# The second block's projections, branch gates and output projection as three passes of high and low parts

## The chip, the cores and the metric

The program runs on one core of a Trainium2 chip. The metric is the device time of one execution, in microseconds. The engines are TensorE (PE; its weight loads are PEld), VectorE (DVE), ScalarE (ACT), GpSimd (POOL) and SyncE (SP, which here only starts transfers).

## What is computed

Two blocks follow one another on x, 512 tokens by 1024 columns, all in float32. The first block has two layers of attention (three kinds of heads) and a gated feed-forward network (FFN). The change is in the second block, cut here to what matters:

```python
u   = modulate(rms_norm(x, norm1_g), sh1, sc1)            # 512 tokens
u_c = modulate(rms_norm(ctx, norm1_g), sh1c, sc1c)        # 256 tokens of context
p, pc = split_cols(u @ w_in), split_cols(u_c @ w_in)
# p[0:4] GLA q, k, v, gate; p[4] 32 columns of decay ranks; p[5:9] mLSTM q, k, v, gate;
# p[9] 16 columns of gates; p[10] 2 x 1024 branch gates
o = bidirectional(gla_scan, ...)                          # 4 heads, dk 128, dv 256, chunks of 64
h = bidirectional(mlstm_scan, ... to_colmajor(p[j]) ...)  # 4 heads, tokens in column order
y_gla = head_rms_norm(o) * silu(p[3])
y_m   = from_colmajor(head_rms_norm(h)) * sigmoid(p[8])
gate_gla, gate_m = split(sigmoid(p[10]))
y = gate_gla * (y_gla @ w_br_gla) + gate_m * (y_m @ w_br_mlstm)
x = x + g1 * (y @ w_out)
x = x + g2 * swiglu(modulate(rms_norm(x, norm2_g), sh2, sc2), w_ffn_in, w_ffn_out)
return rms_norm(x, final_g)
```

Each of the two directions of a scan runs over the context first and then over the 512 tokens. The largest matrix products have a contraction of 1024, that is eight k tiles of 128.

## The kernel before

Every engine has its own instruction list, written out in order by one Python function per engine; semaphores order the engines among each other. There is no planner.

In the first block, and in the FFN of both blocks, a float32 product is three matmuls on numbers in the type fp32r: an operand a is split into a high part (a rounded to fp32r) and a low part (a minus its high part, rounded to fp32r), and high x high + high x low + low x high are added up in PSUM. In the second block, from its projections to its output projection, the products are plain fp32 matmuls on x and weights as they come. `mm` (L754) issues every matmul.

The weights of the second block come over the SyncE queue (`load`, L1405, which walks through `second_pieces`, L473) into three slots of `ring`, each of 4096 columns; a piece holds q, k and v of a head, or its gate, or the four 128-column parts of one branch step, or half of the output weights. TensorE goes in this order:

- It transposes ctx, sums the squares of ctx (`norm_sums`), spreads the inverse roots, computes the 32 decay-rank columns for x and for ctx, then the eleven projections of GLA head 0 (`PROJECTIONS`, L497: q; k of the context, ("k", 0); k of x, ("k", 1); six 128-token tiles of v, two of the context and four of x; two gate tiles of 128 columns).
- In each of the four GLA heads it does the decay inputs of this head and, put between them and the two scans (`gla_scan`, L1217), the projections of the next head: q behind the first decay inputs, both k and v 0 and 1 behind the second, v 2 behind the first scan's key transposes, v 3 between the state updates, v 4 behind them, v 5 and a gate in the second scan, the other gate ahead of `head_outputs`. A generator per unit (`steps` in `projections`, L1161) lets single k tiles be placed between other matmuls.
- In GLA head 3 these are the projections of mLSTM head 0, on x in column order. GpSimd permutes four of the eight k tiles of the normed x and VectorE the other four (`permute`, L562).
- Then the 16 gate columns, the gate rows (running sums and maxima on four partitions, on VectorE), q and k of mLSTM head 1, and the four mLSTM heads (`mlstm_scan`, L1306), again with the next head's projections between. Head 3 has no next head.
- The branch stage: for each of eight column tiles a gate (`branch_gates`, L1347), the product of the GLA output with its branch weights, a second gate, the product of the mLSTM output. Then eight jobs of the output projection, and the FFN.

ScalarE moves the results out of PSUM in the same order (`evacuate`, L1747), between the decay exponentials (`decay_exponents`, L1772: a chain of activations that waits for VectorE's running sums) and the head's norm. In it q of the next head is evacuated inside the first direction's chain, ("k", 0) inside the second's, and ("k", 1) and v behind it. VectorE norms x and ctx (`norm_apply`), makes the decays, the states, the state updates out of PSUM, and the products with the gates. GpSimd has little to do in the second block: it starts the transfer of ctx, permutes, and subtracts for the first FFN piece (`first_low`, L666).

Of the kernel before, what the change touches and what calls it, by code (L numbers as in the profile page):

```python
# [81 lines left out]
def build(nc, A, out):  # L82
    ctx = ExitStack()
    with ctx:
# [8 lines left out]
        spare = sb("spare", [P, 2, KT * P])  # L93
# [49 lines left out]
        with ExitStack() as mixing:  # L143
            U = mixing.enter_context(nc.sbuf_tensor("U", [P, KT, 768], F32))
            R = mixing.enter_context(nc.sbuf_tensor("R", [P, 26624], F32))
            ring = mixing.enter_context(nc.sbuf_tensor("ring", [P, NSLOT, SLOT], F32))

        with ExitStack() as parts:
# [3 lines left out]
            ring_parts = parts.enter_context(nc.sbuf_tensor("ring_parts", [P, NSLOT, SLOT], mybir.dt.float32r))  # L152
        with ExitStack() as stacked:
            stacked.enter_context(nc.sbuf_tensor("U_under", [P, KT, 768], F32))
            stacked.enter_context(nc.sbuf_tensor("R_under", [P, QK_AT], F32))
            QKP = stacked.enter_context(nc.sbuf_tensor("QK_parts", [P, 20, S], mybir.dt.float32r))
        xn = U[:, :, 256:768]
# [12 lines left out]
        wL = sb("wL", [P, 2, FP], FR)  # L170

# [142 lines left out]
        ctxin = R[:, 14208:16256].rearrange("p (t c) -> p t c", t=CT)  # L314
        ctxT = R[:, 16256:18304].rearrange("p (k c) -> p k c", k=KT)
        U0 = U[:, :, 0:256]
# [32 lines left out]
        setup = sem("setup")  # L349
        sq_ready, folded = sem("sq_ready"), sem("folded")  # L350
# [122 lines left out]
        def second_pieces():  # L473
            w = A["w_in_2"][0]
            yield lambda i: [(slot(i, KT, 32), cols(w, O_LR, O_LR + 32))]
            for o in (O_GLA, O_ML):
                for h in range(NH2):
                    if o is O_ML and h == 1:
                        yield lambda i: [(slot(i, KT, 16), cols(w, O_GATES, O_GATES + 16))]
                    gate = lambda i, h=h, o=o: [(slot(i, KT, DV), cols(w, o[3] + h * DV, o[3] + (h + 1) * DV))]  # L480
                    if o is O_ML and h == 0:
                        yield gate
                    yield lambda i, h=h, o=o: [
                        (slot(i, KT, DK, 0), cols(w, o[0] + h * DK, o[0] + (h + 1) * DK)),
                        (slot(i, KT, DK, KT * DK), cols(w, o[1] + h * DK, o[1] + (h + 1) * DK)),
                        (slot(i, KT, DV, 2 * KT * DK), cols(w, o[2] + h * DV, o[2] + (h + 1) * DV))]
                    if o is O_GLA or h > 0:
                        yield gate
            for m in range(KT):
                yield lambda i, m=m: [  # L490
                    (slot(i, KT, P, n * KT * P), cols(src, a + m * P, a + (m + 1) * P))
                    for n, (src, a) in enumerate(((w, O_BR), (A["w_br_gla_2"][0], 0), (w, O_BR + D), (A["w_br_mlstm_2"][0], 0)))]
            for j in range(2):
                yield lambda i, j=j: [(slot(i, KT, 512), cols(A["w_out_2"][0], j * 512, (j + 1) * 512))]


        PROJECTIONS = [("q", 0), ("k", 0), ("k", 1)] + [("v", t) for t in range(6)] + [("gate", 0), ("gate", 1)]  # L497
# [59 lines left out]
        vtmp2 = R[:, 12288:12800].rearrange("p (a c) -> p a c", a=1)  # L557
        BR = R[:, 8192:8192 + 4096].rearrange("p (k c) -> p k c", k=KT)
# [3 lines left out]
        def permute(pg, e, k, scratch):  # L562

            pg.do(e.tensor_copy(scratch.rearrange("p (c r) -> p c r", r=8), xn[:, k, :].rearrange("p (r c) -> p c r", c=64)))
            pg.do(e.tensor_copy(xn[:, k, :], scratch))
# [13 lines left out]
        def _(pool):  # L579
# [143 lines left out]
            pg.more(x_ready, KT)  # L723
            pool.dma_start(ctxin, A["ctx_2"][0].rearrange("(t p) c -> p t c", p=P)).then_inc(ctx_in, 16)
# [6 lines left out]
            pg.seen[sq_ready] = (2 * L + 1) * KT  # L731
# [7 lines left out]
        def _(pe):  # L739
# [38 lines left out]

            def norm_sums(src, nt, ks, bank=None):

                if bank is None:
                    bank = ab.fill(pe)
                for k in ks:
                    pp.more(sq_ready)
                    for t in range(nt):

                        ins = nc.tensor.matmul(bank[:, t:t + 1], src(k)[:, t * P:(t + 1) * P], ones[:, 0:1],
                                               start=k == 0 and t == 0, stop=k == KT - 1, skip_group_check=True)
                    if k == KT - 1:
                        ins.then_inc(a_full, 1)  # L790
                return bank
# [343 lines left out]
            Xc = lambda k: U0[:, k, :]  # L1135

# [3 lines left out]

            spread_roots(S)
            pe.wait_ge(ctx_in, 16)
# [7 lines left out]
            norm_sums(Xc, CT, range(KT))  # L1150
            spread_roots(256)
            pp.more(xn_ready, KT)
            i = weights()
# [1292 lines left out]
```

## Time and profile before

| | us |
|---|---|
| median of 3 runs | 3038.78 |
| lowest and highest of them | 3037.37, 3041.61 |
| the profiled execution | 3035.83 |
| its span (first to last instruction) | 3034.0 |
| TensorE busy in the span | 2849.8 (94%) |
| second block, ahead of its FFN | 1579 to 2627 |

The profile is of one execution, and all positions below are microseconds from the start of its span. A record of the timeline joins instructions that follow one another: it shows the start, the time to the end of the last, the engine, line and operation, output and inputs by name with their sizes, the count, and in brackets the idle time before it with what ended it. "PE L754 ... x32" is 32 matmuls. An fp32 matmul leaves two records, one in fp32r leaves one. PEclk is the granted TensorE clock as a share of full speed.

### The profile page before, as it was taken

The numbers are of one execution on the slowest core, as the hardware profiler recorded it, in microseconds if no ns is written. First come the engines' busy times: TensorE is split into PE (matmuls) and PEld (weight loads), VectorE is DVE, ScalarE is ACT, GpSimd is POOL, SyncE is SP. The second block draws the span as 40 slices with busy tenths as digits, with TensorE's granted clock in tenths as the row PEclk, the third lists the DMA queues.
The fourth block names the chain that finished last, engine by engine and source line by source line (L and its number), as shares of the span: only waits on it lengthen the run. The fifth ranks groups of instructions, "written<-read, shape, count | busy, mean of one in ns | idle before, by whom it ended". The sixth has DMA issues, their size and how long they took to land.

```text
span 3034.0 us, 33407 instructions
## 1 busy us (share of the span) xinstructions
PE 2849.8 (94%) x13064; PEld 2038.8 (67%) x13064; DVE 1240.7 (41%) x1736; ACT 972.5 (32%) x1634; POOL 753.7 (25%) x600
## 2 busy tenths in 40 slices
PE   7988999999999899999989999798998999899997
PEld 6866668887896675888765555446665444488886
DVE  2758445443263853554231333425333100333322
ACT  5468422222344861222221334332222000122221
POOL 5565403346544650234650000100000000100000
PEclk9999999999999999999999999899998999899999
DMA  5230024545422002455551110111112231133331
GB/s 126 91 64 1 19 82 123 138 131 142 122 86 85 5 18 56 111 138 135 142 154 49 42 39 18 29 31 53 35 35 56 56 83 56 42 97 98 90 95 66
DMA packets 383948, 230.26 MB, mean 76 GB/s; under 512 B 9292, under 2 KB 378060, under 8 KB 383792
## 3 DMA queue, kind: packets, MB, share of 16 engines
q1 hardware_dynamic: 381040, 223.04, 26.5%
q0 software_dynamic: 2224, 2.99, 0.9%
q8 instruction: 104, 1.70, 0.2%
q10 hardware_dynamic: 528, 2.10, 0.2%
q14 instruction: 52, 0.43, 0.0%
HBM read 226.01 MB, written 2.10 MB: 75 GB/s over the span
## 4 chain that ended last, share of the span: by engine, by line
PE 76%; ACT 8%; DVE 7%; DMA 6%; issue 2%; POOL 0%; SPq 0%; ACTq 0%; DVEq 0%; POOLq 0%
PE ps L754 65%; PE scores L754 8%; DMA raws<-in_w_down 5%; PE ps L910 1%; ACT wH L1685 1%; DVE R L1957 1%; DVE spare L1967 0%; ACT spare L1547 0%; ACT U L1524 0%; DMA ring<-in_w_in 0%; ACT R L1552 0%; DVE QK_parts L1947 0%; ACT R L1520 0%; PE ps L858 0%; ACT U_parts L1476 0%
## 5 line engine op out<-in xcount | busy, mean ns | idle before, releaser
L754 PE MATMUL ps<-xH,wH 128*128 128x512 f32 x992 | 391.5, 395 | 0.0
L754 PE MATMUL ps<-xH,wL 128*128 128x512 f32 x992 | 386.5, 390 | 0.0
L754 PE MATMUL ps<-xL,wH 128*128 128x512 f32 x992 | 386.1, 389 | 0.0
L1685 ACT ACTIVATE wH<-raws 128x2048 fp32r<-128x2048 f32 (+1 forms) x114 | 192.9, 1692 | 504.3 <-PE ps L754 312.1
L2154 DVE TENSOR_TENSOR wL<-raws,wH 128x2048 fp32r<-128x2048 f32 (+1 forms) x113 | 233.0, 2062 | 280.5 <-ACT wH L1685 280.4
L754 PE MATMUL ps<-R 128*64 128x128 f32 (+6 forms) x1768 | 272.6, 342 | 30.3 <-issue 4.5
L754 PE MATMUL ps<-U,ring 128*128 128x512 f32 (+4 forms) x640 | 269.3, 573 | 8.2 <-ACT R L1767 8.2
L754 PE MATMUL ps<-R,ring 128*128 128x512 f32 x624 | 271.3, 593 | 2.9 <-DVE R L2378 1.6
L663 POOL TENSOR_TENSOR U<-U 128x512 f32<-128x512 f32 x12 | 19.5, 1627 | 1023.4 <-ACT U L1480 1023.4
L754 PEld LDWEIGHTS ps<-R 128*64 128x64 f32 (+2 forms) x1768 | 171.1, 165 | 147.3 <-issue 86.9
L680 POOL TENSOR_TENSOR spare<-spare,cvec 128x1024 f32<-128x1024 f32 x64 | 125.3, 1958 | 560.5 <-DMA spare<-in_w_ada 560.5
L754 PE MATMUL ps<-ring_parts,U_parts 128*128 128x256 f32 (+1 forms) x1440 | 208.1, 284 | 12.9 <-DVE ring_parts L2009 6.7
L754 PEld LDWEIGHTS ps<-R,ring 128*128 128x128 f32 x624 | 118.2, 190 | 151.6 <-issue 147.7
L754 PEld LDWEIGHTS ps<-xH,wL 128*128 128x128 f32 x992 | 186.3, 188 | 39.7
L754 PEld LDWEIGHTS ps<-U,ring 128*128 128x128 f32 (+2 forms) x640 | 118.2, 188 | 140.8 <-issue 125.1
L754 PEld LDWEIGHTS ps<-xL,wH 128*128 128x128 f32 x992 | 186.5, 188 | 38.9 <-issue 1.0
L754 PEld LDWEIGHTS ps<-xH,wH 128*128 128x128 f32 x992 | 186.5, 188 | 38.3 <-issue 1.0
L754 PE MATMUL ps<-hH,wH 128*128 128x512 f32 x528 | 209.9, 398 | 1.5 <-DVE wL L2154 1.5
L754 PE MATMUL ps<-hH,wL 128*128 128x512 f32 x528 | 207.0, 392 | 0.0
L754 PE MATMUL ps<-hL,wH 128*128 128x512 f32 x528 | 206.8, 392 | 0.0
L754 PEld LDWEIGHTS ps<-ring_parts,U_parts 128*128 128x128 f32 x1440 | 193.9, 194 | 14.1 <-issue 11.8
L682 POOL TENSOR_TENSOR spare<-spare 128x512 f32<-128x512 f32 (+2 forms) x192 | 198.3, 1033 | 15.0
(367 smaller groups left out, 4159.2 us busy)
## 6 DMA issues: line engine op xcount, KB each, us to landing
raws<-in_w_gate_up SPq DMA_DIRECT2D x88, 512.0 KB, 5.5
ring<-in_w_in SPq DMA_DIRECT2D x34, 1024.0 KB, 6.3
spare<-in_w_ada SPq DMA_DIRECT2D x64, 512.0 KB, 4.1
raws<-in_w_down SPq DMA_DIRECT2D x32, 704.0 KB, 6.1
raws<-in_w_ffn_in SPq DMA_DIRECT2D x44, 512.0 KB, 5.1
ring<-in_w_in SPq DMA_DIRECT2D x32, 512.0 KB, 6.2
raws<-in_w_ffn_out SPq DMA_DIRECT2D x16, 704.0 KB, 4.6
ring<-in_w_o SPq DMA_DIRECT2D x6, 896.0 KB, 5.6
```

What stands on the lines that cost most here:

```text
L663: pg.do(nc.gpsimd.tensor_tensor(xn[:, 0, :], xn[:, 0, :], xn[:, k, :], ALU.add), folded)
L680: pg.do(nc.gpsimd.tensor_tensor(w_, w_, bc(cvec[:, :, ADA[a][1]], P, 2), ALU.mult))
L682: pg.do(nc.gpsimd.tensor_tensor(w[:, 0:n_ * P], w[:, 0:n_ * P], w[:, n_ * P:2 * n_ * P], ALU.add), ada_summed if n_ == 1 else None)
L754: return nc.tensor.matmul(o, a, b, start=first, stop=last)
L910: ins = nc.tensor.transpose(bank[:, s_ * P:(s_ + 1) * P], PX[a % 4][:, c, s_ * P:(s_ + 1) * P], ident[:, :])
L1685: ap.do(f(wH[:, g % 2, 0:n], raws[:, g % 2, 0:n], ACT.Copy), wh_ready)
L1957: vp.do(v.tensor_reduce(nmax[:, n:n + 2], SP[a % 2][:, :, :], AX.X, ALU.max, negate=True), s_max)
L2154: vp.do(v.tensor_tensor(wL[:, g % 2, 0:n], raws[:, g % 2, 0:n], wH[:, g % 2, 0:n].bitcast(F32), ALU.subtract), wl_ready)
```

## The change

The second block's projections, narrow jobs, branch gates and output projection become three passes of high and low parts. The two products of the branch stage with w_br_gla and w_br_mlstm stay plain fp32.

- The weights come in 36 pieces of 128 x 2048 (256 columns for each of eight k tiles): q and k of a head, v, gate, in this order by head (v and gate of mLSTM head 0 ahead of its q and k), then eight pairs of branch gates and four quarters of the output weights. A piece goes to place 0 or 1 in turn (`PLACE`), and from the branch stage on to places 0, 2, 3, of which 2 and 3 lie in `R`. A place holds the raw piece, and its high and low parts in `ring_parts` or `R_parts`.
- ScalarE rounds piece j + 1 (`second_part`) behind an evacuation of piece j: behind the second unit of a q/k or v piece, behind the first of a gate piece; in the branch stage behind every second gate. GpSimd makes all low parts (`split_piece`), and both parts of the 32 and 16 narrow columns (`split_small`).
- x is normed into a high part (`x_high`, ScalarE) and a low part (`u_low`, VectorE). ctx is normed ahead of its transposes, by ScalarE (squares with a sum, root, scaled copy), and ScalarE writes it twice out of PSUM; VectorE subtracts.
- `permute` copies both parts of each k tile. `PROJECTIONS` goes q, ("k", 1), ("k", 0). In the entry the rank columns of the context come behind q and k of x.
- The branch sums are split into `BR_HIGH` and `BR_LOW`. The first FFN piece of the second block waits for the last piece in place 0 (the second output quarter) instead of the last output weights.

The diff, cut to its core:

```diff
+        SECOND = ([(name, h) for h in range(NH2) for name in ("qk", "v", "gate")]
+                  + [("v", NH2), ("gate", NH2), ("qk", NH2)]
+                  + [(name, h) for h in range(NH2 + 1, 2 * NH2) for name in ("qk", "v", "gate")])
+        N_PROJ = len(SECOND)
+        SECOND += [("branch", m) for m in range(KT)] + [("out", j) for j in range(4)]
+        PLACE = [j % 2 for j in range(N_PROJ)] + [(0, 2, 3)[j % 3] for j in range(KT + 4)]
-        PROJECTIONS = [("q", 0), ("k", 0), ("k", 1)] + ...
+        PROJECTIONS = [("q", 0), ("k", 1), ("k", 0)] + ...
@@ permute (GpSimd and VectorE)
-            pg.do(e.tensor_copy(scratch.rearrange(...), xn[:, k, :].rearrange(...)))
-            pg.do(e.tensor_copy(xn[:, k, :], scratch))
+            for part in (x_high(k), u_low(k)):
+                pg.do(e.tensor_copy(scratch.rearrange(...), part.bitcast(F32).rearrange(...)))
+                pg.do(e.tensor_copy(part, scratch))
@@ GpSimd
+            def split_piece(j):
+                raw_, high, low = place_parts(PLACE[j])
+                if j == 0:
+                    pool.wait_ge(piece_in[0], 16 * len(second_dmas(0)))
+                    pg.do(nc.gpsimd.tensor_copy(high, raw_))
+                else:
+                    pool.wait_ge(second_high, j)
+                pg.do(nc.gpsimd.tensor_tensor(low, raw_, high.bitcast(F32), ALU.subtract), piece_split)
+            for j in range(4, SECOND.index(("gate", NH2))):
+                split_piece(j)
             pool.wait_ge(head_in, NH2)
             for k in range(POOL_TILES):
                 permute(pg, nc.gpsimd, k, ptile)
             pg.also(u_permuted)
+            for j in range(SECOND.index(("gate", NH2)), len(SECOND)):
+                split_piece(j)
@@ TensorE
+            def parts_steps(o, a, b, on_tile=None):
+                for k in range(KT):
+                    if on_tile:
+                        on_tile()
+                    (ah, al), (bh, bl) = a(k), b(k)
+                    mm(o, ah, bh, k == 0, False)
+                    mm(o, ah, bl, False, False)
+                    yield mm(o, al, bh, False, k == KT - 1)
@@ projections, steps
-                    i = at_slot[part]
+                    j = SECOND.index(("qk" if name in "qk" else name, h))
+                    pe.wait_ge(piece_split, j + 1)
                     bank = ab.fill(pe)
...
+                    for ins in parts_steps(o, a, b):
+                        done = ins
                         yield
+                    done.then_inc(a_full, 1)
+                    read_second[j] = (a_full, ab.n)
@@ branch gates and output
+                j = N_PROJ + m
+                pe.wait_ge(piece_split, j + 1)
+                parts_job(ab, lambda b: b[:, :], piece_columns(j, n * P, P), XP)
...
+                parts_job(db, lambda b: b[:, :], piece_columns(j, m % 2 * P, P), lambda k: (BR_HIGH[:, k, :], BR_LOW[:, k, :]))
@@ SyncE
+            def load_second(j):
+                i = PLACE[j]
+                if last[i] is not None:
+                    sp.wait_ge(*read_second[last[i]])
...
+                for dst, src in second_dmas(j):
+                    sp.dma_start(dst, src).then_inc(piece_in[i], 16)
@@ ScalarE
+            def second_part(j):
+                i = PLACE[j]
+                landed[i] += 16 * len(second_dmas(j))
+                act.wait_ge(piece_in[i], landed[i])
+                raw_, high, _ = place_parts(i)
+                ap.do(f(high, raw_, ACT.Copy), second_high)
             def evacuate(h, *jobs):
...
+                    evacuate_one(h, name, m)
+                    j = SECOND.index(("qk" if name in "qk" else name, h))
+                    units[j] += 1
+                    if units[j] == (1 if name == "gate" else 2):
+                        second_part(j + 1)
@@ ScalarE, branch gates
                 ap.also(gate_ready)
+                if n % 2 or n == 2 * KT - 2:
+                    second_part(N_PROJ + (n + 1) // 2 + (n >= 2 * KT - 2))
@@ VectorE
-            norm_apply(lambda k: gm[:, 0, k:k + 1], lambda k: mod[:, sh1 + k, 0:1])
-            vp.more(ctx_ready)
-            norm_apply(lambda k: gm[:, 1, k:k + 1], lambda k: mod[:, sh1 + k, 1:2], U0, ctxT, CT)
+            norm_into_parts(lambda k: gm[:, 0, k:k + 1], lambda k: mod[:, sh1 + k, 0:1], u_low, x_high, context_root)
+            for k in range(0, KT, 2):
+                two = slice(k, k + 2)
+                vp.do(v.tensor_tensor(spare_parts[:, two, :], ctxT[:, two, :], UP[:, two, 0:256].bitcast(F32), ALU.subtract), xn_ready)
...
-                vp.do(v.tensor_tensor(BR[:, m, :], BR[:, m, :], vtmp2[:, 0, :], ALU.add), br_ready)
+                vp.do(v.tensor_tensor(PTb[:, 0, :], PTb[:, 0, :], PTb[:, 1, :], ALU.add))
+                split(BR_HIGH[:, m, :], BR_LOW[:, m, :], PTb[:, 0, :], br_ready)
```

## Rows read from the trace of the kernel before

**Rows 1.** the page's busy time by engine: us, share of the span, instructions

```profile
PE 2849.8 (94%) x13064; PEld 2038.8 (67%) x13064; DVE 1240.7 (41%) x1736; ACT 972.5 (32%) x1634; POOL 753.7 (25%) x600
```

**Rows 2.** windows view: stretch, us, busy us (xcount) of PE, PEld, DVE, ACT, POOL, PEclk, DMA, GB/s

```profile
1603.00:1668.10 65.10, 64.35 (x210) 37.12 (x209) 8.34 (x19) 7.33 (x14) 0.00 (x0) 0.97 0.18 49
1842.00:1928.50 86.50, 80.41 (x313) 46.82 (x312) 32.36 (x54) 31.87 (x51) 0.00 (x0) 0.98 0.13 37
1928.50:2010.60 82.10, 62.96 (x266) 37.70 (x266) 37.31 (x62) 30.34 (x48) 7.64 (x8) 0.88 0.01 1
...
2137.30:2218.80 81.50, 78.95 (x307) 51.33 (x306) 28.19 (x71) 19.15 (x35) 0.00 (x0) 1.00 0.14 39
2363.00:2570.00 207.00, 205.39 (x479) 90.63 (x477) 15.98 (x24) 10.46 (x17) 0.00 (x0) 1.00 0.26 71
```

**Rows 3.** timeline, matmuls: start us, us, engine line operation, xcount [idle before <-releaser]

```profile
2570.01 55.20 PE L754 MATMUL ps<-R,ring 128*128 128x512 f32 x128 [1.62 <-DVE R L2378]
...
1643.08 7.07 PE L754 MATMUL ps<-ring,U 128*128 128x256 f32 x32
...
2700.11 0.39 PE L754 MATMUL ps<-xH,wH 128*128 128x512 f32 x1
...
2702.83 0.39 PE L754 MATMUL ps<-xH,wH 128*128 128x512 f32 x1
...
60.48 1.84 PE L754 MATMUL ps<-ring_parts,U_parts 128*128 128x256 f32 x14
62.16 0.28 PE L754 MATMUL ps<-ring_parts,xL 128*128 128x256 f32 x1
```

**Rows 4.** groups by line and form, the splitting of weights: xcount, busy us, mean ns

```profile
L1472 ACT ACTIVATE ring_parts<-ring 128x2048 fp32r<-128x2048 f32 x18 | 34.5, 1917 | 6.3 <-DMA ring<-in_w_in 5.4 <-DVE wL L2154 0.3
...
L643 POOL TENSOR_TENSOR ring_parts<-ring,ring_parts 128x2048 fp32r<-128x2048 f32 x17 | 79.1, 4653 | 85.4 <-ACT ring_parts L1472 85.1
```

**Rows 5.** timeline of the head at 1842 us

```profile
1842.02 0.69 PE L754 MATMUL ps<-R,C 32*128 32x256 f32 x2
...
1856.32 12.21 PE L754 MATMUL ps<-U,ring 128*128 128x256 f32 x32 [4.19 <-ACT R L1767]
...
1869.29 0.39 ACT L1524 ACTIVATE R<-ps 128x256 f32<-128x256 f32 x1
...
1875.27 1.05 PE L754 MATMUL ps<-R 128*128 128x128 f32 x8
...
1902.79 0.70 PE L754 MATMUL ps<-R 64*128 64x256 f32 x4
...
1915.76 4.89 PE L754 MATMUL ps<-R 128*128 128x256 f32 x24 [0.75 <-DVEq L56]
...
1920.58 7.13 PE L754 MATMUL ps<-U,ring 128*128 128x512 f32 x16
...
1925.33 1.52 DVE L2250 TENSOR_SCALAR R<-R,rsg 128x256 f32<-128x256 f32 x4
```

**Rows 6.** timeline at the start of the last feed-forward network

```profile
2631.57 1.91 ACT L1685 ACTIVATE wH<-raws 128x2048 fp32r<-128x2048 f32 x1 [3.22 <-PE ps L754]
...
2632.41 0.49 DVE L2135 TENSOR_SCALAR R<-R,mod 128x512 f32<-128x512 f32 x1
...
2633.62 4.50 POOL L670 TENSOR_TENSOR wL<-raws,wH 128x2048 fp32r<-128x2048 f32 x1 [12.30 <-ACT wH L1685]
...
2633.72 4.68 DVE L2135 TENSOR_SCALAR R<-R,mod 128x512 f32<-128x512 f32 x1
```

**Rows 7.** timeline at the permutation

```profile
1944.39 0.60 DVE L564 COPY R<-U 128x512 f32<-128x512 f32 x1
...
1948.86 8.61 PE L754 MATMUL ps<-ring,U 128*128 128x256 f32 x32 [17.25 <-DVEq L56]
```

**Rows 8.** timeline at the end of the gate rows

```profile
2069.60 1.01 PE L1303 MATMUL ps<-ident,R 4*128 4x4 f32 x8 [6.83 <-ACT R L1844]
```

**Rows 9.** timeline of the mLSTM head at 2137 us

```profile
2170.72 0.69 DVE L2352 TENSOR_TENSOR R<-R 128x512 f32<-128x512 f32 x1 [2.09 <-ACT R L1864]
```

More of the change, by code:

```diff
@@ new lines, in second_dmas @@
+        def second_dmas(j):
+            (name, h), w = SECOND[j], A["w_in_2"][0]
+            dst = place_parts(PLACE[j])[0]
+            if name == "branch":
+                return [(dst[:, :, n * P:(n + 1) * P], cols(w, O_BR + n * D + h * P, O_BR + n * D + (h + 1) * P)) for n in range(2)]
+            if name == "out":
+                return [(dst, cols(A["w_out_2"][0], h * 256, (h + 1) * 256))]
+            o, h = (O_GLA, O_ML)[h // NH2], h % NH2
+            if name == "qk":
+                return [(dst[:, :, n * DK:(n + 1) * DK], cols(w, o[n] + h * DK, o[n] + (h + 1) * DK)) for n in range(2)]
+            n = 2 if name == "v" else 3
+            return [(dst, cols(w, o[n] + h * DV, o[n] + (h + 1) * DV))]
@@ L498, in build, with branch_raw @@
+        read_second, branch_read = [None] * len(SECOND), []
+        def branch_raw(m, n):
+            return slot(1, KT, P, m % 2 * (SLOT // 2) + n * KT * P)
+        PROJECTIONS = [("q", 0), ("k", 1), ("k", 0)] + [("v", t) for t in range(6)] + [("gate", 0), ("gate", 1)]
         N_CONST = 4 + L * (6 + 1 + 4)
@@ L777, in _ @@
             pe.wait_ge(setup, 2)
[L779 to L791, printed above, removed]
             def two_sums(bank, total, last):
@@ L1254, in head_outputs @@
                     ins.then_inc(d_full, 1)
-            first = projections()
-            for name, m in PROJECTIONS:
+            first = projections(0)
+            for name, m in PROJECTIONS[:2]:
+                run(first(name, m))
+            pp.more(xn_ready, KT // 2)
+            parts_job(ab, lambda b: b[0:32, 0:256], small(LR_AT, 2 * RANK), XcP)
+            pe.wait_ge(tab_in, 80)
+            for name, m in PROJECTIONS[2:]:
                 run(first(name, m))
@@ L1278, in _ @@
                 head_outputs()
[L1281 to L1285 removed]
+            pe.wait_ge(gates_split, 1)
+            parts_job(ab, lambda b: b[0:16, 0:256], small(GATES_AT, 16), XcP)
+            parts_job(ab, lambda b: b[0:16, :], small(GATES_AT, 16), XP)
             gates_out = ab.n
@@ L1413, in load_ffn @@
                 up_down = FFN_W[l]
-                sp.wait_ge(*read_by[base + (before[l] - base - 1) // NSLOT * NSLOT])
+                if l < L:
+                    sp.wait_ge(*read_by[base + (before[l] - base - 1) // NSLOT * NSLOT])
+                else:
+                    sp.wait_ge(*read_second[max(j for j in range(len(SECOND)) if PLACE[j] == 0)])
                 for q in range(NF):
```

301 lines of the change are left out of this document (169 added, 132 removed).

## The prediction

> **What bounds the kernel now.** I read the page first: TensorE is busy for 94% of the span [rows 1]. Then I cut the second block (1579 to 2627 us) into stages with the windows view [rows 2]: in the first projections and the branch stage the matmul records fill the window (64.35 of 65.1 us, 205.39 of 207). In the scan stages they nearly do (80.41 of 86.5 us in a GLA head, 78.95 of 81.5 in an mLSTM head), and only around the permutation is there a hole (62.96 of 82.1). So a cheaper matmul shortens the first kind of stage one for one. In a scan stage one has to follow the chain: there projections fill the time in which ScalarE and VectorE work on the decays.
>
> The prices [rows 3]: an fp32 matmul is two records, one of 512 columns 55.20/128 = 0.43 us, so 0.86 per k tile; one of 256 columns 7.07/32 = 0.22, so 0.44. In fp32r, 512 columns come every 2.72/12 = 0.227 us, three passes 0.68; 256 columns every 1.68/14 = 0.12, three passes 0.36. A k tile of 512 columns gains 0.18, one of 256 gains 0.08.
>
> **The change, part by part.** Each of eight heads has 32 k tiles of 512 columns (q, k, two gates) and 56 of 256 (k of the context, six v): 5.8 + 4.5 = 10.3 us less matmul, 82 in all. Sixteen branch gates (128 k tiles) give 23, the output projection (64) 11.5, the two narrow jobs 4: 121 us of work leave TensorE. What is added per 1 MB piece of weights stands between its landing and its first matmul: ScalarE's rounding, 1.92 us, and GpSimd's subtraction, 4.65 [rows 4], for 36 pieces. Neither engine is full (ScalarE 31.9 of 86.5 us in a head [rows 2]). What counts is where in ScalarE's order the rounding stands.
>
> *Entry.* x is now normed into two parts, so VectorE's last tile comes at about 1605 to 1607 instead of 1596 (an estimate: one more 128x512 subtraction per tile, 0.69 as in [rows 9], and collisions with GpSimd, below), but TensorE no longer waits for the context's norm before x's jobs. Behind it stand q and k of x (2 x 5.4), the narrow job and k of the context (2 x 2.9), six v (17.3), two gates (10.9): 44.8, and some 4 for the first v piece (rounded only after two evacuations) and a slow clock: head 0 begins at 1656, not 1668. -12, bounds -17 (no collision) and -6.
>
> *GLA heads 0 to 2.* This is where I expect the work saved to be lost. A head begins at 1842.02 [rows 5]. Its k of the context waits 4.19 us for ScalarE's evacuation of q, which stands behind the decay chain, and k's own evacuation comes at 1869.29, 27.3 us into the head: ScalarE reaches it by its exponentials, not by TensorE's. The rounding of the next head's v piece now stands right behind that evacuation, and TensorE's v job waits for rounding and subtraction: 27.7 + 1.9 + 4.6 = 34.2 us into the head. In the kernel before both first v jobs were done at 33.25 (1875.27). TensorE now idles from about 25 to 34.2, and such an idle time brings the slow clock: after the 4.19 us wait, 32 records of 256 and 512 columns took 12.21 us for the 10.4 that [rows 3] give. So v0 and v1 (5.8, and 2 for the clock) end at 42, 8.7 later than before. Back come: v2 0.6, the scan with v3 and v4 1.7, v5 0.6, the second scan with a gate between its pairs (1902.79 to 1915.76, 13 us) 2.2. The last gate's 1.5 is mostly not regained: the head's norm chain ends at 1926.85, 6.3 after that gate starts, and the gate now takes 5.4. That is 5.7 back of 8.7: each head +3, three heads +9. Bounds: 0 (the clock stays up and the chain starts earlier, since ScalarE evacuates the last gate sooner) and +18 (6 a head).
>
> *GLA head 3.* The permutation copies both parts: GpSimd's 7.64 us [rows 2] and VectorE's 4.4 (1944.39 to 1948.8, the end of TensorE's 17.25 us wait [rows 7]) double, and VectorE starts later behind GpSimd's copies: +6. The rest of the head returns 5.5. Sum +0.5, bounds -5 and +3.
>
> *Gate rows.* The narrow jobs and q start the chain 3.7 earlier. But from about 2041 VectorE works through scans and row operations without a pause, and TensorE waits for the end of it (2069.60, 6.83 idle [rows 8]). Two subtractions (q/k and v of mLSTM head 1) fall into this stretch. That GpSimd holds VectorE up is in the trace: while GpSimd subtracted for 4.50 us, a VectorE operation that began 0.10 later took 4.68 where its like took 0.49 [rows 6]. Two such stops cost up to 9. Sum +5, bounds -4 (no stop) and +6.
>
> The Trainium skill (SBUF — State Buffer, on the port pair that VectorE and GpSimd share) says that the pair is an exclusive lock, held for the whole instruction, against VectorE operations in a two-port mode or with two SBUF inputs. By that rule the scans and additions of the gate rows are stopped as the one above was, and those that read PSUM are not; without it this stage would be -4 instead of +5 and the forecast some 15 us lower.
>
> *mLSTM heads 0 to 2.* Here q and k are evacuated without a chain before them, so v is rounded at 9 and subtracted at 15.5 us into the head; v0 starts 15.6 in, 17.2 before. The gate piece's subtraction then covers VectorE's multiplication of the scores (2170.72, 33.4 into the head [rows 9]), which without it would come 3 us earlier. I get: second direction starting 3.8 earlier, its v jobs and gate another 2.8, the last gate lost to the norm chain as above: -6.5 a head, -4.5 for head 0, whose q and k lie in the stage before. -17.5, bounds -22 and -9. Head 3 has no projections: 0.
>
> *Branch.* Fifteen gates outside other waits gain 1.4 each: 21. Each next pair is rounded behind the evacuation of the second gate: 0.8 + 1.9 + 4.65 = 7.4 after it, while the one job in between takes 6.9: 0.6 lost seven times. -16.5, bounds -21 and -12.
>
> *Output projection.* 64 k tiles at 0.18: -11.5, and two more VectorE operations (0.6 and 0.69 [rows 7, 9]) ahead of it, on top of the 1.62 us wait [rows 3]: -10.3, bounds -11.4 and -9. The last rounding waits for a transfer, and the squares of x queue behind it, with four jobs of cover.
>
> *FFN start.* Its first piece loads after the second output piece instead of after the last, so ScalarE's 3.22 us wait [rows 6] goes, and with it GpSimd's subtraction and VectorE move up: -3.2, bounds -3.5 and 0. Next is GpSimd's 4.50 us.
>
> Sum: -12 + 9 + 0.5 + 5 - 17.5 - 16.5 - 10.3 - 3.2 = -45. The profiled execution took 3035.83 (span 3034.0 and 1.8 around it), 2.95 below the median of the three runs: 2991 against it, **2994** against the median. The bounds add up to -84 and -9.
>
> **The rivals.** *All of the matmul time comes home.* If ScalarE and GpSimd were ready everywhere, 3039 - 121 + 6 (the doubled permutation) = 2924. For it: their low load; against it the fixed place of the rounding behind an exponential chain. *The v wait and the port are milder:* GLA heads at 0 to -3, no stops in entry and rows: -45 - 15 - 14 = 2965. For it: collisions hang on microseconds. *The heads give nothing:* mLSTM lands at its weak bound and each GLA head at +6: -45 + 9 + 8 = 3011. *Slower:* GpSimd's subtractions stop VectorE wherever they fall. Twenty-one of them lie in seven heads, at 4.5 us; I count some five on a path already. From ten more that hit the decay chains or the state updates on, the gain is gone; if all hit, 16 x 4.5 = 72 more, 3066. Against it: by the walk above most subtractions fall over state updates, and these read PSUM; no row here shows such an operation stopped.
>
> **How the numbers follow.** Forecast 2994, own range 2977 to 3008: 0.58. Milder, about 2965: 0.14. All home: 0.05. Heads give nothing, about 3011: 0.13. Slower: 0.06; gains and stops cancel: 0.04. With the neighbours: 2965 to 3015 for 8 in 10. What one measurement can tell from no change is 0.2%, 6 us: faster 0.90, same 0.04, slower 0.06.
>
> **What would show it.** Right: in each GLA head TensorE idle some 9 us ahead of v0, released by GpSimd; head length near 89; a slow clock behind it; mLSTM heads near 75; a branch step 25.3 instead of 27.5 with a short GpSimd wait in it; out job 5.45; VectorE operations of over 4 us in the gate rows. Wrong: GLA heads shorter than 84 (the v piece is ready earlier than I read it), or VectorE stops of 4 us inside the state updates (the port reaches further).

## The result and the profile after

In six runs each, side by side, the changed kernel took 3023.79 us (3016.52 to 3033.69) and the kernel before 3040.20: ratio 0.9941, 95% interval 0.9914 to 0.9968. Forecast was 2994, range 2965 to 3015: the kernel became faster, by some two fifths of what was forecast. The two profiled executions, 3035.83 and 3016.52, differ by 19.3, so the stages of the two traces account for the whole difference. Busy time by engine, on the page of after:

```profile
PE 2761.5 (92%) x13958; PEld 2138.9 (71%) x13958; DVE 1288.8 (43%) x1755; ACT 1052.2 (35%) x1687; POOL 932.5 (31%) x648
```

Against [rows 1] TensorE is busy for 88 us less, and 69 of them came back as idle time. Part of that busy time ran at a lower clock than before. Counted at full clock (an estimate: the busy time of the two traces times the clock granted in it) the work is 2673 us for 2792. So 119 us of work left TensorE, as the prediction had it (121): 69 became idle time, 30 went into slower matmuls, and 19 shortened the execution.

| stage, from TensorE's first matmul of it to that of the next | before | after | change | forecast |
|---|---|---|---|---|
| up to GLA head 0 | 1668.1 | 1652.2 | -15.9 | -12 |
| GLA heads 0 to 2 | 260.4 | 275.4 | +15.0 | +9 |
| GLA head 3 and gate rows, up to the mLSTM heads' row selection | 152.0 | 161.8 | +9.9 | +5.5 |
| mLSTM heads, up to the first branch product | 274.8 | 267.7 | -7.1 | -17.5 |
| branch, up to the first output matmul | 214.8 | 204.2 | -10.5 | -16.5 |
| output projection, up to the sums of squares | 56.8 | 48.2 | -8.6 | -10.3 |
| start of the FFN, up to its first matmul | 12.4 | 10.6 | -1.8 | -3.2 |
| rest | 394.7 | 394.6 | -0.2 | 0 |

The windows of the stages that answer to [rows 2]: GLA head 2, GLA head 3, mLSTM head 1, branch (columns as there):

```profile
1836.84:1927.55 90.71, 74.15 (x402) 55.41 (x401) 35.93 (x54) 37.58 (x54) 13.61 (x3) 0.91 0.12 35
1927.55:2013.30 85.75, 59.02 (x330) 42.38 (x329) 43.76 (x70) 33.97 (x50) 27.00 (x18) 0.82 0.09 25
2145.00:2223.86 78.86, 72.87 (x396) 59.79 (x393) 30.87 (x71) 24.88 (x38) 13.73 (x3) 0.96 0.15 41
2357.00:2561.20 204.20, 193.91 (x616) 115.51 (x616) 29.55 (x40) 28.06 (x25) 45.04 (x10) 0.99 0.30 83
```

Only in the branch is TensorE still full. A GLA head's matmul records fill 74 us where they filled 80, and the head is 4 us longer; the granted clock is lower in every one of the scan stages (0.91 for 0.98, 0.82 for 0.88, 0.96 for 1.00).

The timeline of the head at 1744.55, where [rows 5] show the one before:

```profile
1771.61 0.38 ACT L1609 ACTIVATE R<-ps 128x256 f32<-128x256 f32 x1
1772.03 1.91 ACT L1850 ACTIVATE ring_parts<-ring 128x2048 fp32r<-128x2048 f32 x1
...
1774.08 4.50 POOL L769 TENSOR_TENSOR ring_parts<-ring,ring_parts 128x2048 fp32r<-128x2048 f32 x1 [37.44 <-ACT ring_parts L1850]
...
1774.91 4.48 DVE L2350 TENSOR_TENSOR R<-R 128x768 f32<-128x768 f32 x1 [2.73 <-ACT R L1906]
1778.64 0.80 PE L815 MATMUL ps<-ring_parts,U_parts 128*128 128x256 f32 x2 [10.07 <-POOL ring_parts L769]
```

This is the chain that the prediction described: k evacuated 27.1 us into the head, rounded, subtracted, and v 0 starts 34.1 in, after 10.07 us of idle TensorE. The VectorE operation beside the subtraction takes 4.48 us; where no subtraction lies beside it, it takes 0.96.

The gate rows have two such stops, and TensorE's wait at their end is 12.02 where [rows 8] show 6.83:

```profile
2044.36 5.42 POOL L769 TENSOR_TENSOR ring_parts<-ring,ring_parts 128x2048 fp32r<-128x2048 f32 x1 [38.77 <-ACT ring_parts L1850]
2045.52 4.80 DVE L2419 TENSOR_TENSOR_SCAN R<-R 4x256 f32<-4x256 f32 x1
...
2064.67 0.68 DVE L2419 TENSOR_TENSOR_SCAN R<-R 4x256 f32<-4x256 f32 x1
2068.87 4.61 POOL L769 TENSOR_TENSOR ring_parts<-ring,ring_parts 128x2048 fp32r<-128x2048 f32 x1 [19.09 <-ACT ring_parts L1850]
2069.16 5.13 DVE L2438 TENSOR_TENSOR R<-R,mrow 4x768 f32<-4x768 f32 x1
2078.41 1.01 PE L1352 MATMUL ps<-ident,R 4*128 4x4 f32 x8 [12.02 <-ACT R L1964]
```

And one stands ahead of the output projection, where the forecast had none; the wait there was 1.62 [rows 3]:

```profile
2554.42 0.69 DVE L2507 TENSOR_TENSOR R<-R,ps 128x512 f32<-128x512 f32 x1 [11.57 <-PE ps L815]
2554.97 4.50 POOL L769 TENSOR_TENSOR R_parts<-R,R_parts 128x2048 fp32r<-128x2048 f32 x1
2555.25 4.76 DVE L2509 TENSOR_TENSOR R<-R 128x512 f32<-128x512 f32 x1
2560.04 0.43 DVE L2271 CAST R_parts<-R 128x512 fp32r<-128x512 f32 x1
2560.50 0.69 DVE L2272 TENSOR_TENSOR R_parts<-R,R_parts 128x512 fp32r<-128x512 f32 x1
2561.25 13.94 PE L815 MATMUL ps<-R_parts 128*128 128x512 f32 x48 [6.87 <-DVE R_parts L2272]
```

The first addition reads PSUM and takes its 0.69; the next, with both inputs in SBUF, starts 0.28 after GpSimd and ends 0.54 after it. Behind the wait 48 matmuls take 13.94 us, the next 48 take 11.04.

### The profile page after: what moved, and what is told of

Read it like the earlier page. It is cut to its first block, busy times and chain, and to the rows that moved or that the text cites. A ratio compares the mean times of both kernels' runs of the same rounds, so it can differ in the third digit from the quotient of the medians.

```text
span 3014.6 us, 35487 instructions
## 1 busy us (share of the span) xinstructions
PE 2761.5 (92%) x13958; PEld 2138.9 (71%) x13958; DVE 1288.8 (43%) x1755; ACT 1052.2 (35%) x1687; POOL 932.5 (31%) x648
## 4 chain that ended last, share of the span: by engine, by line
PE 70%; ACT 10%; DVE 9%; DMA 6%; POOL 2%; issue 2%; SPq 0%; ACTq 0%; DVEq 0%; POOLq 0%
PE ps L815 60%; PE scores L815 7%; DMA raws<-in_w_down 5%; PE ps L957 1%; ACT wH L1770 1%; POOL ring_parts L769 1%; DVE R L2083 1%; POOL R_parts L769 1%; ACT ring_parts L1850 1%; ACT R L1916 0%; DVE spare L2093 0%; DVE R L2341 0%; ACT U L1609 0%; DVE R L2256 0%; DVE R L2259 0%
## 5 line engine op out<-in xcount | busy, mean ns | idle before, releaser
L815 PE MATMUL ps<-ring_parts,U_parts 128*128 128x256 f32 (+1 forms) x1936 | 313.9, 291 | 32.3 <-POOL ring_parts L769 20.4
L769 POOL TENSOR_TENSOR ring_parts<-ring,ring_parts 128x2048 fp32r<-128x2048 f32 x28 | 128.6, 4591 | 621.7 <-ACT ring_parts L1850 621.6
L815 PEld LDWEIGHTS ps<-ring_parts,U_parts 128*128 128x128 f32 x1936 | 279.1, 198 | 46.1 <-POOL ring_parts L769 21.6
L815 PE MATMUL ps<-R 128*64 128x128 f32 (+6 forms) x1768 | 280.3, 348 | 29.6 <-DVE R L2359 4.6
L815 PE MATMUL ps<-U_parts,ring_parts 128*128 128x512 f32 (+2 forms) x720 | 218.9, 395 | 14.8 <-ACT R L1884 8.3
L815 PE MATMUL ps<-R,ring 128*128 128x512 f32 x496 | 216.1, 593 | 1.3 <-DVEq L56 1.3
L815 PEld LDWEIGHTS ps<-R,ring 128*128 128x128 f32 x496 | 93.9, 190 | 113.1 <-issue 110.4
L815 PEld LDWEIGHTS ps<-U_parts,ring_parts 128*128 128x128 f32 (+1 forms) x720 | 135.0, 193 | 54.3 <-issue 18.2
```

Of the source, the lines that this page charges most:

```text
L769: pg.do(nc.gpsimd.tensor_tensor(low, raw_, high.bitcast(F32), ALU.subtract), piece_split)
L815: return nc.tensor.matmul(o, a, b, start=first, stop=last)
```

## The experiments

Each time is a median beside runs of the kernel before on the same chip; compare the ratios to it. The changed kernel stood only in the first group, with 0.9968 (0.9955 to 0.9980), and 0.9941 in its first six runs; so between groups a difference of some 0.3% is read from the traces and not from the medians.

**The changed kernel again.**

> The changed kernel once more, as the measure for the three runs beside it. Expected: 3016 to 3034 us, median 3024, as in its first six runs; GLA heads of 91 to 92 us, a TensorE wait of some 12 us at the end of the gate rows. If its spread comes from the clock, the granted clock of its runs (0.948 to 0.957 before) falls as the time rises.

3025.89 us (3021.07 to 3028.39), profiled at 3026.69: GLA heads 93.5, 92.9, 92.6 and a wait of 12.63 us at the end of the gate rows. The heads are 1 us longer than expected, the rest is as expected. Two executions of one kernel differ by 10 us in the GLA and mLSTM heads; 6 of them are in the first mLSTM head, which took 84.5 us at a clock of 0.88 here and 78.2 at 0.96 in the first trace.

**Short subtractions everywhere.**

```diff
-                pg.do(nc.gpsimd.tensor_tensor(low, raw_, high.bitcast(F32), ALU.subtract), piece_split)
+                for k in range(KT - 1):
+                    pg.do(nc.gpsimd.tensor_tensor(low[:, k, :], raw_[:, k, :], high[:, k, :].bitcast(F32), ALU.subtract))
+                pg.do(nc.gpsimd.tensor_tensor(low[:, KT - 1, :], ..., ALU.subtract), piece_split)
```

> GpSimd subtracts each piece in eight instructions of 128x256 instead of one of 128x2048; the same numbers, nothing left out. Theory 1 (GpSimd keeps VectorE out for a whole instruction): the VectorE operations of 4 to 5 us fall to under 1.5 us; the gate rows come back by 7.5 us (two stops of 4.1 and 4.2 us), mLSTM heads by 1 to 3 us each, the start of the output projection by 4 us, the GLA heads by 0 because their stop ends before TensorE needs its result: about 15 us in all, near 3009. A piece is split some 0.5 us later, 0 to 2 us lost. Theory 2 (both engines share a bandwidth, and the sum of bytes counts): VectorE still loses some 3.5 to 4 us per piece, spread over more operations, and the time stays at 3024.

3066.93 us, ratio 1.0106 (1.0093 to 1.0119): 41 us slower than the changed kernel. Both theories missed the time. The timeline of a GLA head and of the branch:

```profile
1782.50 6.13 POOL L770 TENSOR_TENSOR ring_parts<-ring,ring_parts 128x256 fp32r<-128x256 f32 x7 [35.50 <-ACT ring_parts L1852]
1783.34 1.51 DVE L2352 TENSOR_TENSOR R<-R 128x768 f32<-128x768 f32 x1 [2.73 <-ACT R L1908]
1788.72 0.72 POOL L771 TENSOR_TENSOR ring_parts<-ring,ring_parts 128x256 fp32r<-128x256 f32 x1
...
2412.10 0.73 PE L817 MATMUL ps<-U_parts,R_parts 128*128 128x512 f32 x1 [2.67 <-POOL R_parts L771]
```

The stop fell to 0.55 us (1.51 for 0.96), so it is the length of GpSimd's instruction that VectorE waits for. But the piece takes 6.9 us for 4.5, and in the branch each pair of gates now waits 2.67 us where it waited 0.49: from the first branch product to the FFN the kernel takes 280.6 us for 263.0. In the whole second block the idle time of TensorE that GpSimd ended is 82 us where the changed kernel beside it has 44, which is the size of the loss: GpSimd's subtraction is on TensorE's path at more places than VectorE's stops are.

**The rounding of v earlier.**

```diff
-                    if units[j] == (1 if name == "gate" else 2):
+                    if units[j] == (1 if name == "gate" or name in "qk" and 0 < h < NH2 else 2):
```

> In the GLA heads ScalarE rounds the next head's v piece behind the evacuation of q (14 us into the head) and not behind that of k of the context (27 us). Nothing is left out. Theory 1 (the place of the rounding costs the GLA heads their gain): TensorE's wait of 8.5 to 10 us ahead of v 0 goes, the first scan starts at 31 to 34 us into the head instead of 41.4, and each of three heads is 5 to 9 us shorter, less some 2 us for the stop of VectorE that now falls into the first direction's chain: about 18 us, near 3006. Theory 2 (a GLA head is bound by the decay and state chain, whatever TensorE does): heads stay at 91 to 92 us, 3024.

3004.82 us, 0.9904 (0.9889 to 0.9920): 21 us under the changed kernel, theory 1. In the head at 1739.0:

```profile
1753.07 1.91 ACT L1850 ACTIVATE ring_parts<-ring 128x2048 fp32r<-128x2048 f32 x1
1755.13 4.55 POOL L769 TENSOR_TENSOR ring_parts<-ring,ring_parts 128x2048 fp32r<-128x2048 f32 x1 [22.46 <-ACT ring_parts L1850]
1755.96 4.53 DVE L2350 TENSOR_TENSOR R<-R 128x768 f32<-128x768 f32 x1 [2.95 <-ACT R L1906]
...
1761.19 0.77 PE L815 MATMUL scores<-U_parts,ring_parts 128*128 128x512 f32 x1 [3.35 <-ACT R L1895]
...
1775.18 1.05 PE L815 MATMUL ps<-R 128*128 128x128 f32 x8
```

The first scan starts 36.2 us in (42.0 in the changed kernel), heads take 85.5 to 85.7 instead of 92.6 to 93.5. The stop now delays the second direction's decays, and TensorE waits 3.35 us for a bank. Without the wait for v a head is 0.7 to 2.1 us shorter than before the change, for 10 us less matmul.

**Idle time filled.**

```diff
+                    if name == "v" and m == 0 and 0 < h < NH2:
+                        bank = ab.fill(pe)
+                        for _ in range(30):
+                            mm(bank[:, :], x_high(0)[:, 0:P], x_high(0), True, True)
+                        pe.wait_ge(piece_split, j + 1)
...
```

> Ahead of the wait for the v piece in GLA heads TensorE does 30 matmuls of 512 columns on x, written into the bank that v 0 overwrites; they change no result and take some 7 us of the idle 8.5 to 10. Theory 1 (the idle time brings the slow clock behind it): the granted clock over v 0 and v 1 goes from about 0.8 to near 1, the two take 6 us instead of 7.4, each head is 1.5 us shorter, 4.5 in all: near 3019. Theory 2 (the fall of the clock has another cause than this wait): no change of the clock behind the wait, 3024. If the extra matmuls bring slow stretches elsewhere, the time rises.

3027.24 us, 0.9977 (0.9962 to 0.9993): no change. The wait ahead of v 0 was 2.81 us instead of 9.45, and v 0 and v 1 took 7.54 us at clock 0.77 instead of 8.13 at 0.70. Filling most of the gap hardly raises the clock behind it, so the slow clock there is not this wait's alone.

**One copy in the permutation** (`for part in (x_high(k),)` for both parts):

> The changed kernel, but the permutation copies only the high part of each k tile of x; the low part stays in row order (left out: its permutation). Theory 1 (the second copy stands on the path): TensorE's wait at the permutation, 24.2 us, is 17 to 18 us again, mLSTM head 0 starts 6 to 7 us sooner, and the time is near 3019 where the changed kernel has 3024 to 3026, ratio to before 0.995 or so. Theory 2 (the gate rows, bound by VectorE, take the gain back): the wait is shorter, the end of the gate rows moves by less than 2 us, no change.

3020.81 us, 0.9939 (0.9923 to 0.9954). TensorE's wait ahead of the permuted x, first in the changed kernel and then here:

```profile
1954.57 0.79 PE L815 MATMUL scores<-ring_parts,U_parts 128*128 128x256 f32 x2 [24.18 <-DVEq L56]
1952.62 0.79 PE L815 MATMUL scores<-ring_parts,U_parts 128*128 128x256 f32 x2 [17.08 <-DVEq L56]
```

The end of the gate rows comes 143.9 us after GLA head 3 began, for 150.9: theory 1 by the traces, and 7 us, which the gate rows pass on in full. The ratio alone does not show it, as the changed kernel had 0.9968 and 0.9941.

**Two passes.** `parts_steps` leaves out the third matmul where the head is not the first; on the early rounding.

> The run with the early rounding of v, and in the projections of every head but the first the third pass (low x high) left out: by the prices of the traces 32 x 0.227 + 56 x 0.12 = 14 us less matmul in each of seven heads, 98 in all. Theory 1 (the scan stages are bound by the decay, state and norm chains, and what TensorE saves there is idle time): GLA heads go from 85.6 to 82 to 85 us, mLSTM heads from 79 to 75 to 79, the whole 10 to 30 us under the 3005 of the early rounding, and TensorE's idle time grows. Theory 2 (TensorE bounds these stages once the wait for v is gone): 10 to 14 us a head, 70 to 95 in all, near 2920.

2984.84 us, 0.9826 (0.9807 to 0.9844): 20 us under the early rounding by the medians and 24 by the ratios, theory 1. The windows of the three GLA heads and the second mLSTM head, first with two passes, then the early rounding with three:

```profile
1656.50:1736.20 79.70, 61.40 (x312) 42.77 (x312) 34.27 (x52) 37.62 (x53) 16.76 (x6) 0.91 0.19 48
1736.20:1819.90 83.70, 65.67 (x314) 46.28 (x313) 35.63 (x54) 37.60 (x53) 13.63 (x3) 0.86 0.13 38
1819.90:1902.80 82.90, 67.28 (x314) 46.76 (x313) 35.89 (x54) 37.61 (x53) 14.45 (x4) 0.83 0.14 38
2135.30:2213.70 78.40, 69.12 (x305) 55.79 (x304) 31.03 (x70) 24.90 (x37) 13.63 (x3) 0.80 0.15 41
```

```profile
1653.40:1739.00 85.60, 74.48 (x400) 55.18 (x400) 33.97 (x52) 37.31 (x53) 16.78 (x6) 0.92 0.15 38
1739.00:1824.50 85.50, 74.13 (x401) 54.99 (x400) 35.99 (x54) 37.63 (x54) 13.68 (x3) 0.92 0.14 38
1824.50:1910.00 85.50, 74.07 (x402) 54.92 (x401) 36.03 (x54) 37.68 (x54) 13.67 (x3) 0.92 0.13 38
2155.90:2234.70 78.80, 72.83 (x394) 59.74 (x393) 30.85 (x70) 24.89 (x37) 13.74 (x3) 0.96 0.15 41
```

A third less projection work shortens GLA head 0, where the clock hardly changes, by 5.9 us. GLA heads 1 and 2 are shortened by 1.8 and 2.6 and the mLSTM head by 0.4; in these TensorE's busy time falls by 7 to 8.5 and by 4, not by 14, because the granted clock is lower too. So at best some 6 of the 14 us come home, and the rest is idle time or slower matmul.

**Six pieces short, and v of the context ahead of the permuted x.** The first takes the eight short instructions only for pieces in `SHORT = [("v", 1), ("v", 2), ("v", 3), ("qk", NH2 + 1), ("v", NH2 + 1), ("out", 1)]`; the second also moves `pp.more(u_permuted, 2)` behind v 0 and v 1.

> The early rounding, and GpSimd's subtraction in eight short instructions for six pieces alone: v of GLA heads 1 to 3, q/k and v of mLSTM head 1, the second quarter of the output weights. Nothing left out. Theory 1 (the stop of VectorE costs where it falls into a chain, the longer subtraction where TensorE waits for it, as in the branch stage): the gate rows end 8 us sooner, each GLA head is 1 to 3 us shorter (its stop of 3.6 us is in the first direction's chain now), the output starts 4 us sooner: 12 to 20 us under the early rounding, 2985 to 2993. Theory 2 (short subtractions cost more than they free in any place, as the run with all of them short came out 41 us slower): 3005 or more.

> As the run with six short pieces, and in GLA head 3 TensorE does v 0 and v 1 of mLSTM head 0, which are tiles of the context and not permuted, ahead of its wait for the permuted x and not behind it. Nothing left out. Theory 1 (these 8 us of matmul stand behind the permutation for no other reason): the first scan of GLA head 3 starts 5 to 8 us sooner, 2978 to 2986. Theory 2 (VectorE, which does half of the permutation, holds the first scan as long): 0 to 2 us.

2993.72 us, 0.9856 (0.9837 to 0.9875), and 3000.69, 0.9878 (0.9860 to 0.9895). The first beats the early rounding, but not where expected. GLA heads stay at 85.4 to 85.5 (one at 82.4). The gate rows end 3.5 us sooner, not 8: VectorE waits for many short instructions, and the q/k piece comes so late that TensorE waits 10.59 us for it (6.04 with the early rounding). And ahead of the output projection the shortened piece was the wrong one, the stop comes from the third quarter:

```profile
2540.91 4.55 POOL L774 TENSOR_TENSOR R_parts<-R,R_parts 128x2048 fp32r<-128x2048 f32 x1
2541.14 4.86 DVE L2279 TENSOR_TENSOR R_parts<-R,R_parts 128x512 fp32r<-128x512 f32 x1
```

The second is no faster: v 0 starts 17.6 us into GLA head 3 instead of 27.0, but the first scan's state updates start at 39.5, for 39.3 before. Theory 2, and a small case of what the two-pass run shows at large.

**Subtractions moved, and two more places.** The first run rounds q/k of mLSTM head 1 behind q of head 0 and puts `act.wait_ge(br_ready, KT)` ahead of the third output quarter; the second sets `POOL_TILES = 5` and rounds v of mLSTM heads 2 and 3 behind q as well.

> The early rounding of v in GLA heads, and two subtractions moved with their whole length: q/k of mLSTM head 1 is rounded behind q of mLSTM head 0 (VectorE idles there for some 20 us), and the third and fourth output quarter only behind the last split of the branch sums. Nothing left out. Theory 1 (what costs is where a whole subtraction meets VectorE's chain): the first stop in the gate rows (4.1 us) and the stop ahead of the output projection (4.1 us) go, the second stop in the rows (4.2 us) stays; TensorE's wait ahead of the output projection is 2 to 3 us instead of 6.9, the whole 6 to 9 us under the early rounding, ratio to before near 0.988. Theory 2 (a stop that goes only uncovers the next wait): 0 to 3 us.

> As the run with moved subtractions; besides, GpSimd permutes five k tiles of x and VectorE three (four and four before), and v of mLSTM heads 2 and 3 is rounded behind the evacuation of q. Nothing left out. Theory 1 (each of these waits is on the path): TensorE's wait at the permutation goes from 24.2 to some 21.7 us, its wait of 1.7 us for GpSimd ahead of v 0 in mLSTM heads goes: 4 to 6 us under the run with moved subtractions. Theory 2 (mLSTM heads are bound by the scan and norm chain, and GpSimd, slowed by VectorE's own operations, ends the permutation as late): 0 to 2 us.

2995.20 us, 0.9867 (0.9849 to 0.9885), and 2991.03, 0.9859 (0.9839 to 0.9879). Ahead of the output the moved subtraction frees VectorE:

```profile
2533.64 0.69 DVE L2510 TENSOR_TENSOR R<-R 128x512 f32<-128x512 f32 x1
2534.36 0.43 DVE L2272 CAST R_parts<-R 128x512 fp32r<-128x512 f32 x1
2534.82 0.69 DVE L2273 TENSOR_TENSOR R_parts<-R,R_parts 128x512 fp32r<-128x512 f32 x1
2535.57 12.62 PE L815 MATMUL ps<-R_parts 128*128 128x512 f32 x48 [2.81 <-DVE R_parts L2273]
```

The wait is 2.81 instead of 6.87, and from the first branch product to the FFN it takes 257.95 us instead of 263.1. In the gate rows the first stop is gone too, but the rounding stands in front of the gate columns on ScalarE and VectorE's chain starts 3 us later: 1 us is left of 4.1. In the second run the wait at the permutation is 24.07 (GpSimd's fifth tile gained nothing), while mLSTM heads take 76.4 and 76.3 us for 78.2 and 78.9: there the 1.74 us wait for GpSimd ahead of v 0 is gone.

**A fourth pass, for the clock.** `parts_steps` adds low x low, in all projections of mLSTM heads 6 and 7 (counted from GLA head 0) or only in v 1 and v 4 of heads 5 to 7.

> As the run with five permuted tiles on GpSimd and the early v in mLSTM heads, and a fourth matmul (low x low) in every k tile of the projections done in mLSTM heads 1 and 2: 32 x 0.227 + 56 x 0.12 = 14 us more matmul work in each of the two. Nothing is left out. It asks what the granted clock in these stages hangs on: it was 1.00 before the change, 0.96 after it with three passes, 0.80 with two. Theory 1 (the less matmul work a stage holds, the lower the clock): 0.98 to 1.00 in the two stages, 80 to 86 us each instead of 76.3, because 3 us of slow clock and 4 us of idle time take up part of the 14. Theory 2 (the clock falls at a place of the order, whatever the projections hold): 0.96 or less again, 86 to 90 us.

> As the run with five permuted tiles, and the fourth matmul only in two v units (v 1 and v 4) of mLSTM heads 1 to 3, which stand among the short matmuls ahead of the stretch where the clock fell to a half: 2 us more work in each of three stages. Theory 1 (more work just ahead of that stretch keeps the clock up): the slow stretches of about 3 and 7 us in these stages go or shrink, and each stage stays at 75 to 76.5 us in spite of the 2 us. Theory 2 (two units are too little or the wrong ones): the same slow stretches, 77 to 78.5 us a stage.

3014.63 us, 0.9927 (0.9904 to 0.9949), and 2991.09, 0.9842 (0.9809 to 0.9875). Windows of the first two mLSTM stages, from one row selection to the next, first with the fourth pass (in q, k and v 0 alone in the first row), then with it in two units:

```profile
2067.60:2149.90 82.30, 78.20 (x429) 65.13 (x428) 31.56 (x70) 23.61 (x36) 13.79 (x3) 0.96 0.14 39
2149.90:2238.30 88.40, 86.01 (x481) 72.59 (x480) 30.29 (x70) 24.88 (x37) 13.76 (x3) 0.96 0.14 36
```

```profile
2072.20:2152.10 79.90, 75.81 (x409) 63.17 (x408) 29.42 (x70) 23.60 (x36) 13.74 (x3) 0.94 0.15 40
2152.10:2227.80 75.70, 71.48 (x410) 58.81 (x409) 30.23 (x71) 24.89 (x37) 13.78 (x3) 1.00 0.16 42
```

With the fourth pass the clock is 0.96 as with three: theory 2 there. With it in two units one stage kept its clock at 1.00 and took 75.7 us with 2 us more work in it, the stage ahead of it 0.94 and 79.9. So the slow stretches are worth about 3 us a stage, and what brings them stays open. These two units, the moved subtractions and the early roundings together make the fastest version of those that leave nothing out, 1.4 to 1.6% under the kernel before and about 1% under the change as made; with and without the two units it is the same within the intervals.

## Why the prediction was wrong

**Right in kind.** Entry, GLA wait, gate rows, branch step and FFN came as described: v 0 at 34.1 us into a head (forecast 34.2), v 0 of an mLSTM head 15.8 in (15.6), two stops in the rows of 4.1 and 4.2 us (9 together), a branch step of 25.4 us (25.3) with a GpSimd wait of 0.49 in it, seven times in the branch. The entry found the favourable bound: one stop of 1.1 us in it, -15.9 for -12. From the first branch product to the end of the last it is -15.8 (-16.5).

**The step that failed** is the one that let the saved matmul time come back inside the scan stages, at the clock of the kernel before. In GLA heads the prediction put the first scan 8.7 us late and gave back 5.7. In heads 0 to 2 the first scan started 8.5, 7.1 and 8.1 late, and each gave back 3.4 up to the outputs of its second scan (24 matmuls). Behind that head 2 gave back 0.5 more, and heads 0 and 1 lost 1.0, since their outputs ran at a lower clock: 6.4 us for the 4.89 that [rows 5] show. So they ended 6.1, 4.7 and 4.2 late. The start of the first scan and the outputs in head 2 (which begins at 1836.84), then the outputs in head 0:

```profile
1878.21 1.05 PE L815 MATMUL ps<-R 128*128 128x128 f32 x8
1915.32 4.89 PE L815 MATMUL ps<-R 128*128 128x256 f32 x24 [0.75 <-DVEq L56]
1730.79 6.42 PE L815 MATMUL ps<-R 128*128 128x256 f32 x24 [0.75 <-DVEq L56]
```

Two of the returns were also larger than the forecast's own prices allow: 16 k tiles of v 3 and v 4 at 0.08 are 1.3 us, not 1.7, and eight of a gate at 0.18 are 1.4, not 2.2. Head 2 shows 0.9 and 1.3 for them. What is missing in the first scan lies in the state updates, where TensorE's update and the two VectorE operations behind it (1.00 us) take turns: a pair with two k tiles of v between takes 1.71 us on average for 1.76, though 0.16 of matmul went. The two-pass run shows the same without the wait: of 14 us of matmul, 5.9 came home in one head, and 1.8 and 2.6 in two heads where the clock fell too. So the early rounding (-7 us a head) brings a head only 0.7 to 2.1 us under what it was before the change.

**The mLSTM heads** were to gain 6.5 us each (4.5 in head 0) and gained 2.5 to 3.3; the last head, forecast at 0, took 1.3 more. In the head at 2145 the second direction started 3.1 us sooner (3.8 forecast), but then took 28.2 us for 27.6, where 2.8 less was forecast. In it the granted clock, 1.00 throughout before [rows 2], falls in a stretch that the matmul records fill:

```profile
2194.00:2196.00 2.00, 2.00 (x15) 1.92 (x14) 0.00 (x0) 0.38 (x1) 0.00 (x0) 0.77 0.00 0
2196.00:2202.00 6.00, 6.00 (x29) 5.78 (x29) 1.39 (x2) 1.61 (x3) 0.00 (x0) 0.51 0.00 0
2202.00:2204.00 2.00, 2.00 (x14) 1.83 (x13) 0.43 (x1) 0.39 (x1) 0.00 (x0) 1.00 0.03 2
```

TensorE's records leave no gap of note from 2187.8 on, 7 us ahead of the fall; the row selections with their short matmuls stand there. Six us at 0.51 (1.2 GHz of 2.4) are 3 us of matmul lost, most of what is missing. In the trace of before the clock does not fall in mLSTM heads 0 to 2 (it does in head 3, which has no projections). In the trace of after such stretches add up to 21 us in these three heads, by the same reckoning 10 us of matmul, and the forecast had no term for them: slow clock stood in it only behind the wait for v and in the entry. That the walk itself was about right is seen where the clock stayed at 1.00: the stage of 75.7 us above, with 2 us more work and 1.7 us less wait in it, against a forecast of 75. What lowers the clock there stays open. The head's last gate gave nothing, as forecast: TensorE waits 1.57 us for the norm behind it.

**The output projection.** The wait ahead of it grew by 5.25 us where 1.3 was forecast. The prediction had the rule (an operation with two inputs in SBUF is held as long as GpSimd's instruction lasts) and applied it to the entry, the gate rows and the mLSTM heads, but not to the end of the branch; ScalarE rounds three pieces in a row at the end of the branch, the third subtraction meets the last addition, and moving it took 4.06 us off the wait. The slow clock behind the wait costs 2.9 us more (13.94 and 11.04 for 48 matmuls): the jobs take 5.44 us at full clock (5.45 forecast), which is 11.5 less for eight, and 8.6 is what the stage shows. In GLA head 3 the doubled permutation was sized right (+6.9 on the wait, +6 forecast; 7.1 by the run with one copy), but the head gave back 3 instead of 5.5, for the same reasons as the others (its outputs took 6.43 us).

**The stops.** That they last as long as the instruction is shown by cutting it: 4.48 us became 1.51. The Trainium skill (SBUF — State Buffer, on the pair of ports that VectorE and GpSimd share) says that the loser is blocked for the whole instruction, and that a VectorE instruction with at most one SBUF input, outside the two-port modes, does not contend; the traces agree, with 4.76 us for the addition of two inputs in SBUF and 0.69 for the one with an input from PSUM, both beside GpSimd's subtractions. The rival that ended on the slow side put the danger in the number of stops. Eleven of 0.6 to 4.2 us add up to 32 us between the entry and the FFN; those in the decays of GLA heads (3.5 each) cost nothing in the changed kernel, since TensorE was waiting for v then.

**The terms as a whole**: GLA +6, GLA head 3 and rows +4, mLSTM +10, branch and output +8, FFN +1.4, entry -4: 26 us that the forecast's -45 has too much. By the rows above some 17 of them are the lower clock where it had held 1.00 before (an estimate: 1.5 in each of GLA heads 0, 1 and 3, 10 in the mLSTM heads, 2.9 in the output projection) and 4 the stop ahead of the output projection; the rest are smaller terms on both sides, the returns of the GLA heads that were put too high among them. Whether the clock would have stayed up with less waiting in these stages no run shows. The rival "the heads give nothing" (3011) was the nearest, and still counted the full branch.

## What to carry to other kernels

Cheaper matmuls pay where TensorE's records fill the window, here the branch and the entry; in a stage where they stand beside a chain of other engines, follow the chain and price each return by the work that really left it, and set a term for a lower clock: here 119 us of work at full clock became 19 us of time. What the saving needs (rounding, subtracting) has a place in another engine's order: move that place before tuning the work itself, as one condition in ScalarE's order was worth 21 us and cutting GpSimd's instructions cost 41. A long GpSimd instruction should be walked along VectorE's whole order, not only along the stage one is looking at.

## What the runs showed of the hardware

GpSimd's subtraction of 128x2048 takes 4.59 us, eight of 128x256 take 6.4 to 7.7; in one place of VectorE's gate rows the eight took 10.1. The granted clock fell to 0.51 in stretches that matmul records filled, in stages whose like had held 1.00, and in the second mLSTM head it was lower with two passes in the projections than with three (0.80, 0.96), but not higher again with a fourth (0.96), and 1.00 with a fourth in two units alone.
